# Moving the norms' sums to eight columns behind the parameters, and every later SBUF buffer by 32 bytes

## The reference, cut to what matters

```
for i in range(2):                       # block one, x is [256, 1024]
    h = rmsnorm(x, norm_mix_pre[i])
    m = ssd_mixer(h, ...) if i == 0 else rglru_mixer(h, ...)
    x = x + rmsnorm(m, norm_mix_post[i])
    h = rmsnorm(x, norm_ffn_pre[i])
    x = x + rmsnorm(conv_ffn(h, ...), norm_ffn_post[i])
for l in range(2):                       # block two
    h = rms_norm(x, norm1_g[l]) * (1 + sc1) + sh1
    ...                                  # attention, gated delta rule, merge
    x = x + gt1 * (merged @ w_out[l])
    h = rms_norm(x, norm2_g[l]) * (1 + sc2) + sh2
    x = x + gt2 * (square(relu(h @ w_mlp1[l])) @ w_mlp2[l])

def rmsnorm(x, w):
    return x * rsqrt(mean(x * x, axis=-1) + EPS) * w
```

## Time and profile before

| | |
|---|---|
| time, median of 2 runs | 1899.05 us (1898.44 to 1899.66) |
| the profiled execution | 1899.01 us, its span 1897.1 us |
| mean granted TensorE clock | 0.989 |
| PE busy | 1831.0 us (97%), 15229 matmuls |
| PEld busy | 1695.7 us (89%) |
| DVE busy | 1292.3 us (68%) |
| ACT busy | 1017.1 us (54%) |
| POOL busy | 29.5 us (2%) |
| DMA | 336.17 MB, mean 177 GB/s |

### The profile page before, as it was taken

How to read it: one execution, slowest core, us unless ns; L and a number is a source line. 1 busy time by engine, 2 the same in 40 slices (tenths; PEclk the granted TensorE clock), 3 DMA queues, 4 the chain that set the end, 5 groups by cost and what they waited for, 6 DMA issues and landing times. The chain is left out here.

```text
span 1897.1 us, 37837 instructions
## 1 busy us (share of the span) xinstructions
PE 1831.0 (97%) x15229; PEld 1695.7 (89%) x15229; DVE 1292.3 (68%) x1997; ACT 1017.1 (54%) x1584; POOL 29.5 (2%) x48
## 2 busy tenths in 40 slices
PE   6999999999999899999999999999998999999999
PEld 6997788889889698998988999999998999989999
DVE  5948777676777976766777756765556866775554
ACT  5646565555466665555565654544445565454443
POOL 0000000000000000000000001000000000100000
PEclk9999999999999999999999999999999999999999
DMA  7540556766774656556634330445453342044543
GB/s 294 183 171 1 188 212 239 269 244 254 262 271 172 226 211 235 215 216 248 246 114 162 134 112 6 174 142 192 177 185 127 134 156 90 24 156 168 188 177 111
DMA packets 44753, 336.17 MB, mean 177 GB/s; under 512 B 4960, under 2 KB 5088, under 8 KB 6624
## 3 DMA queue, kind: packets, MB, share of 16 engines
q1 hardware_dynamic: 38736, 277.89, 40.2%
q0 software_dynamic: 4608, 50.33, 7.0%
q10 hardware_dynamic: 1296, 6.33, 0.9%
HBM read 333.48 MB, written 1.05 MB: 176 GB/s over the span
## 5 line engine op out<-in xcount | busy, mean ns | idle before, releaser
L667 DVE TENSOR_TENSOR w_lo<-raw,w_hi 128x1024 fp32r<-128x1024 f32 x526 | 639.5, 1224 | 415.4 <-ACT w_hi L658 405.6
L658 ACT ACTIVATE w_hi<-raw 128x1024 fp32r<-128x1024 f32 x526 | 554.2, 1059 | 624.3 <-PE unit L689 397.2
L687 PE MATMUL unit<-h_hi,w_hi 128*128 128x256 f32 x2656 | 758.5, 286 | 27.9 <-DVE h_lo L2088 7.5
L688 PE MATMUL unit<-h_lo,w_hi 128*128 128x256 f32 x2656 | 750.7, 283 | 0.0
L689 PE MATMUL unit<-h_hi,w_lo 128*128 128x256 f32 x2656 | 750.6, 283 | 0.0
L687 PEld LDWEIGHTS unit<-h_hi,w_hi 128*128 128x128 f32 x2656 | 506.6, 191 | 38.6 <-issue 25.7
L688 PEld LDWEIGHTS unit<-h_lo,w_hi 128*128 128x128 f32 x2656 | 507.0, 191 | 1.3
L689 PEld LDWEIGHTS unit<-h_hi,w_lo 128*128 128x128 f32 x2656 | 506.5, 191 | 0.0
L688 PE MATMUL acc<-mv_lo,w_hi 128*128 128x256 f32 x640 | 180.1, 281 | 0.0
L687 PE MATMUL acc<-mv_hi,w_hi 128*128 128x256 f32 x640 | 180.1, 281 | 0.0
L689 PE MATMUL acc<-mv_hi,w_lo 128*128 128x256 f32 x640 | 180.1, 281 | 0.0
(11 more groups left out here) (417 smaller groups left out, 1984.3 us busy)
## 6 DMA issues: line engine op xcount, KB each, us to landing
raw<-w_in SPq DMA_DIRECT2D x263, 1024.0 KB, 4.8
ada_ring<-ada_in POOLq DMA_DIRECT2D x32, 1536.0 KB, 7.6
h<-rows_in ACTq DMA_DIRECT2D x5, 512.0 KB, 3.7
keep<-gates_in ACTq DMA_DIRECT2D x1, 1280.0 KB, 9.6
par<-par_in ACTq DMA_DIRECT2D x1, 1257.0 KB, 12.0
x<-x_in SPq DMA_DIRECT2D x2, 512.0 KB, 7.3
out<-x SPq DMA_DIRECT2D x4, 256.0 KB, 2.3
con<-con_in ACTq DMA_DIRECT2D x1, 950.0 KB, 7.0
```

The costliest lines, as they stand in the source:

```text
L658: act(half(w_hi, c, k), raw[c % RAW][:, CW // 2 * k:CW // 2 * (k + 1)], ACT.Copy).then_inc(S("high_parts"), 1)
L667: tt(half(w_lo, c, k), raw[c % RAW][:, CW // 2 * k:CW // 2 * (k + 1)], half(w_hi, c, k).bitcast(f32), ALU.subtract).then_inc(S("chunk_spli ...
L687: mm(out, w, m, start=first, stop=False)
L688: mm(out, w, ml, start=False, stop=False)
```

## The change

The declaration of `sums` moves from behind `tmp` to behind `par`, and it has one set of eight columns in place of two. `stat` loses its first argument: all norms use the same set, columns 0 to 5 for those after a stage, 6 and 7 for those before one. No instruction is added, removed or moved on any engine, and no wait changes: PE, DVE, ACT, POOL and SP have the same rows in the same order. What changes is addresses (bytes in the partition, as both programs have them):

| buffer | start before | start after | moved | start modulo 64, before / after |
|---|---|---|---|---|
| raw to par | 16512 to 82048 | the same | 0 | 0 / 0 |
| sums | 133536 | 92128 | | 32 / 32 |
| con | 92128 | 92160 | +32 | 32 / 0 |
| ada_ring | 100768 | 100800 | +32 | 32 / 0 |
| rstd | 128416 | 128448 | +32 | 32 / 0 |
| tmp | 129440 | 129472 | +32 | 32 / 0 |
| ident_r (and fold_r to gsc) | 133760 | 133728 | -32 | 0 / 32 |
| keep | 139136 | 139104 | -32 | 0 / 32 |
| late, w_hi0 | 182496 | 182464 | -32 | 32 / 0 |
| w_hi1, w_lo0, w_lo1 | 190688, 198880, 207072 | 190656, 198848, 207040 | -32 | 32 / 0 |

```diff
         par = sb("par", [P, NPAR])
+        sums = sb("sums", [P, 8])
         con = sb("con", [P, NCON])
...
         tmp = sb("tmp", [P, 4, T])
-        sums = sb("sums", [P, 2, 8])
         cact = sb("cact", [P, 8])
...
-        def stat(n, k):
+        def stat(k):
 
-            return sums[:, n % 2, k:k + 1]
+            return sums[:, k:k + 1]
...
-                act(spare[:, s], source[:, s], ACT.Square, accum_out=stat(k, 3 * m + b % 2)).then_inc(S("norm_steps"), 1)
+                act(spare[:, s], source[:, s], ACT.Square, accum_out=stat(3 * m + b % 2)).then_inc(S("norm_steps"), 1)
...
-                ts(diag[:, m, :], ident, stat(n, 6 + m), None, ALU.mult).then_inc(S("norm_factors"), 1)
+                ts(diag[:, m, :], ident, stat(6 + m), None, ALU.mult).then_inc(S("norm_factors"), 1)
```

More of the change, by code:

```diff
@@ L501, in act_post @@
                 s = slice(512 * b, 512 * (b + 1))
-                act(spare[:, s], source[:, s], ACT.Square, accum_out=stat(k, 3 * m + b % 2)).then_inc(S("norm_steps"), 1)
+                act(spare[:, s], source[:, s], ACT.Square, accum_out=stat(3 * m + b % 2)).then_inc(S("norm_steps"), 1)
                 if b % 2:
-                    total = stat(k, 3 * m + 1)
+                    total = stat(3 * m + 1)
                     ac.wait_ge(S("norm_factors"), 4 * k + 3 + m)
                     ac.wait_ge(S("norm_steps"), post_step(k, SUM_AT[b]))
-                    act(total, total, ACT.Ln, bias=stat(k, 3 * m + 2), scale=1.0 / D).then_inc(S("norm_steps"), 1)
+                    act(total, total, ACT.Ln, bias=stat(3 * m + 2), scale=1.0 / D).then_inc(S("norm_steps"), 1)
                     ac.wait_ge(S("norm_steps"), post_step(k, SUM_AT[b] + 1))
@@ L515, in act_pre @@
                 ready(m)
-                act(spare[:, 1024 * m:1024 * (m + 1)], xt[:, m, :], ACT.Square, accum_out=stat(n, 6 + m)
+                act(spare[:, 1024 * m:1024 * (m + 1)], xt[:, m, :], ACT.Square, accum_out=stat(6 + m)
                     ).then_inc(S("norm_steps"), 1)
                 ac.wait_ge(S("norm_steps"), pre_step(n, 3 * m + 1))
-                act(stat(n, 6 + m), stat(n, 6 + m), ACT.Ln, bias=one("eps"), scale=1.0 / D).then_inc(S("norm_steps"), 1)
+                act(stat(6 + m), stat(6 + m), ACT.Ln, bias=one("eps"), scale=1.0 / D).then_inc(S("norm_steps"), 1)
                 ac.wait_ge(S("norm_steps"), pre_step(n, 3 * m + 2))
-                act(stat(n, 6 + m), stat(n, 6 + m), ACT.Exp, scale=-0.5).then_inc(S("norm_steps"), 1)
+                act(stat(6 + m), stat(6 + m), ACT.Exp, scale=-0.5).then_inc(S("norm_steps"), 1)
         def x_updated(eng, stage):
@@ L546, in product @@
                 if b % 2 == 0:
-                    ts(stat(k, 3 * m + 2), stat(k, 3 * m), 1.0 / D, EPS, ALU.mult, ALU.add).then_inc(S("norm_factors"), 1)
+                    ts(stat(3 * m + 2), stat(3 * m), 1.0 / D, EPS, ALU.mult, ALU.add).then_inc(S("norm_factors"), 1)
                 if not biased:
@@ L552, in update @@
                 s = xt[:, b // 2, 512 * (b % 2):512 * (b % 2 + 1)]
-                return stt(s, mw[:, b, :], stat(k, 3 * (b // 2) + 1), s, ALU.mult, ALU.add)
+                return stt(s, mw[:, b, :], stat(3 * (b // 2) + 1), s, ALU.mult, ALU.add)
             product(0)
```

## The result

The changed kernel takes 1872.62 us, the median of 2 runs (1869.01 to 1876.22), against 1899.05: a ratio of 0.9864, with an interval of 0.9817 to 0.9911. So the prediction was wrong: addresses do move the time, and by more than I allowed.

A forecast was written before the change was run, and what follows sets the result against it. The prediction took PE, busy for 97% of 1897.1 us, as the bound. Its terms, 0 + 0 + 0 + 0 on the profiled 1899.01 us (median of the runs 1899.05), gave 1899.0 us, range 1888 to 1908.

The forecast's parts named there:

- What bounds the kernel: Whole kernel: PE, busy for 97% of 1897.1 us, sets the time; ACT and DVE wait for it.
- The pace therefore depends on something that is set when PE starts after a stop: Dense PE stretches, 116.8 to 119.9 ns per matmul: pace set at a restart, not by addresses or other SBUF readers.
- the term of the buffers that start 32 bytes earlier: Moved buffers, in the fp32r matmuls of `three`: taken as 0, within bounds of -17 and +14 us.
- the second kind: Buffers starting 32 past a multiple of 64 bytes; moving or stationary in `three`, no visible difference, 286 against 287 ns.
- the unseen case: Matmuls of `three` with both operands at a multiple of 64, which no row shows; taken as 0.
- The lower bound: 10080 fp32r matmuls going from the middle pace, 118.5 ns, to the fastest row, 116.8: 1.7 ns each, -17 us.
- The slow bound: 10080 fp32r matmuls going from the middle pace, 118.5 ns, to the slowest, 119.9: 1.4 ns each, +14 us.
- rival 2: Dense stretches change pace, in some stages and not in others; between 1882 and 1913 us, chance 0.14.
- rival 3: Every matmul of `three`: operands that start together stream faster, 113.7 ns, -48 us, so 1851 us; chance 0.04.
- Rival 3's figure from the Trainium skill: fp32r matmuls of 256 columns at the page's bf16 rule, 109.2 ns: 94 us given back, so 1805 us.
- Rival 4: Every matmul of `three`: PE's stream and weight load, or ACT's write, collide; 123.0 ns, 45 us, so 1944; chance 0.04.
- Sums, DVE, ACT, fp32 matmuls, DMAs: Norms, DVE and ACT instructions, fp32 matmuls and loads of con and ada_ring at new addresses: each taken as 0.

The follow-up runs named there:

- e1: Kernel before with only the weight buffers (w_hi, w_lo, late) starting 32 bytes earlier, at 182464; 1865.48 us, ratio 0.9822.
- r2: Repeat of e1, the same program, against the kernel before; 1862.77 us, ratio 0.9816.
- e4: Kernel before with weight buffers 32 bytes later, w_hi at 182528, distance 128 from the activations; 1906.81 us, ratio 1.0034.
- e11: Kernel before with activations 32 bytes later and weights unmoved at 182496, distance 64; 1862.36 us, ratio 0.9806.
- e8: Kernel before with activations 64 bytes later and w_hi at 182464, distance 0; 1905.66 us, ratio 1.0034.
- e9: e1 with 32 unused columns between w_hi and w_lo, high weights at distance 64, low at 192; 1853.22 us, 0.9759 of the kernel before.
- p2_probe: p1_probe with separate distances for high and low parts, 144 matmuls a block; both at 64 gave 113.3 ns in nine of twelve blocks, 117.8 in three.
- e3: Kernel before with one shared set of sums and eight unused columns behind it, so no other buffer moves; 1899.31 us, ratio 1.0001.
- e2: Changed kernel with w_hi and w_lo put back at 182496, all other shifts kept; 1896.09 us, 0.9984 of the kernel before.
- p1_probe: PE alone running the matmuls of `three`, not the kernel's computation, weight-to-activation distances 0 to 480 in steps of 32; 113.3 to 120.0 ns per matmul.
- p3_probe: p1_probe with 128, 64 and 32 stationary columns at four distances; with 64 columns, 113.3 ns at distance 0 and 119.0 at 64.

## Why the prediction was wrong, point by point

- **What bounds the kernel: right.** PE did, and nearly all that was won, 28 to 29 of 30.0 us, came from the time from one of its matmuls to the next.
- **"The pace therefore depends on something that is set when PE starts after a stop, such as the instant, and not on the addresses": the step that failed.** The first half holds: one program ran `mlp_0` at two paces (e1 and r2). The second half does not follow from it. Two stages with equal addresses and unequal paces show that something beside the addresses takes part; they say nothing about what other addresses would do, and the trace of before has one distance only. Runs showed that the distance sets which paces there are, and that something at a restart, or at one late step, picks among them. In the sum this step is the term of the buffers that start 32 bytes earlier, which I put at 0; it measured -28 us.
- **Which property of an address matters: wrong.** I sorted buffers by their start modulo 64, one at a time. e4 has all at multiples of 64 and takes 1906.81 us; e11 leaves the weights on an odd 32 and takes 1862.36. What counts is a relation between the two operands of a matmul. "So it makes no visible difference whether the second kind is the moving or the stationary operand" compared two rows with the same distance but for its sign, and by the mean length of a matmul, which moved by 1% (286 to 283 ns) from before to after where the pace of `mlp_1` moved by 5.5%.
- **The bounds: too narrow.** I bounded the unseen case from the rows of the seen ones, 116.8 to 119.9 ns. These were draws from one set. The layout asked for is another set, with 113.3 in it. The lower bound, 1.7 ns on each of 10080 matmuls or -17 us, met a measured 2.8 ns and -28 us. It also rested on a count that reads low: the fastest row, 116.8, is 117.3 from start to start. The slow bound did hold: of the slowest layouts, e8 has a mean step of 119.9 ns and e4 of 119.1, and they take 6 and 8 us more than the kernel before beside them.
- **The rivals.** By its own signs it was rival 2 (`mlp_1` and `ffn0` changed, `mlp_0` and `ssd_in` hardly), at a price outside rival 2's bounds, because rival 3's mechanism, operands at a certain place to each other, is real. Rival 3 had 113.7 as a pace for the case and 1851 us as its time. The pace was about right, though it came from mirroring the scatter of the rows and not from a cause, so that is luck; and e9 comes near that time with 1853.22, but the changed kernel has it in some stages only. The better forecast from the same rows was to give rivals 2 and 3 together much more than 0.18, since all 10080 matmuls of the sum took a relation of operands that no row showed.
- **Rival 3's figure from the Trainium skill.** Page "TensorE: Matmul & The Clock Gate", section "Wait — 56ns, not 53.3ns?", came to 109.2 ns for 256 columns. No block or stage of fp32r matmuls here was faster than 113.3.
- **Rival 4, slower: its mechanism exists in part.** PE's stream and its weight load do get in each other's way. The worst distance costs 120.0 ns, not the 122.3 from which it would have decided; only one block of p2_probe, with high weights at 64 and low at 0, came to 122.1.
- **Sums, DVE, ACT, fp32 matmuls, DMAs: right**, at 0 each as far as seen (e3 for the sums; for the rest the small rows above, and e2's 3 us or less for all of them together).

## What to carry to other kernels

A declaration that pads SBUF can change every matmul that reads a buffer behind it. Where fp32r matmuls with a weight load each are the bound (no other type was tried here), try the start of the stationary buffer against that of the moving one in steps of 32 bytes through 256, as one kernel or one small probe, with several restarts for each distance, and write the best distance down where the buffers are declared. Bound a case that the trace does not show from outside its rows, not from their scatter: equal addresses with unequal paces prove a second cause, not the absence of the first.

## What the runs showed of the hardware

- For fp32r matmuls of 256 columns with a 128-column load before each, the step lies between 113.3 and 120.0 ns at granted clock 1.00, by the two operands' distance modulo 256 bytes (p1_probe, distances 0 to 480). Blocks at 64 and 192 reached 113.3; none at 56, 60, 68 or 72 did, nor at any other distance tried. With high and low weights at distances of their own one block had 122.1. At 2.4 GHz, 113.3 ns are 272 cycles and 120.0 are 288.
- A pace holds to the nanosecond over long stretches, and another can follow a restart: at 64, nine blocks of twelve fell on 113.3 and three on 117.8, with nothing changed but the instant. It can also change without a stop, after one step of 160 ns in e1's `ssd_in`. With high weights at 64 and low weights at 192 the stages of e9 shown above kept the fast pace.
- The weight load is part of it: moving either operand's buffer alone changes the pace (e1, e11), and from 128 to 64 stationary columns the fast distance moves from 64 to 0, with half the output rows beside it (p3_probe). The Trainium skill, page "SBUF — State Buffer", section "Who interferes with whom", calls PE's two read ports, one for the moving operand and one for LDWEIGHTS, independent. Whatever holds for the ports, in time the two reads are not independent for fp32r: with the same instructions and no other engine at work, 113.3 against 120.0 ns by the distance alone (p1_probe).
- Open: what in TensorE or in its reads of SBUF makes these sets, what at a restart or a late step picks from them, why the same stage mostly picks alike, and whether other types of matmul have such sets.
